# Dense logits of one layer section in a single visit, four places for row maxima, lambda's sums ahead of them

## The chip, the cores and the metric

The kernel runs on one core of one Trainium2 chip. The metric is the device time of one execution in microseconds (us). Three runs of the kernel before gave 357.63, 357.84 and 358.26 us; their median is 357.84. TensorE (PE) multiplies matrices and transposes, VectorE (DVE) and ScalarE (ACT) do the elementwise work, GpSimd (POOL) does the rotations, some square roots and small loads, and SyncE (SP) issues the loads of the weights.

## The reference

The program computes two layers (`DEPTH = 2`) of a streaming encoder on 256 tokens of width 1024. Each layer normalises its input, sends it through one input projection, mixes tokens in two groups of heads, gates, projects back, normalises and adds; then a per-layer embedding is gated and added. The group that matters here is the dense one, group B, differential attention with 4 heads and 2 maps for each head:

```python
logits = jnp.einsum('bqhcd,bshcd->bchqs', qb, k).astype(jnp.float32) * (HEAD_DIM ** -0.5)
logits = jnp.where(allowed, logits, NEG_INF)
probs = jax.nn.softmax(logits, axis=-1)
attn = (probs[:, 0] - lam * probs[:, 1]).astype(v.dtype)
...
lam = (jnp.exp(jnp.sum(lambda_q1[i] * lambda_k1[i])) - jnp.exp(jnp.sum(lambda_q2[i] * lambda_k2[i])) + lam_init)
```

Allowed keys are those of the query's chunk of 64 tokens and of the chunks before it. Group A is sparse: an indexer scores the keys, the best 64 are kept (top-k), and a softmax runs over them. The outputs are float32.

## The kernel before

**Tiling.** The 256 tokens are two row blocks of 128 (b = 0 and 1). Weights come in pieces of two 128-row slices by 512 columns, 512 KB each, called units. Every unit is split into a rounded part `w_hi` (copied by ACT) and its remainder `w_lo` (subtracted by DVE), and each product is three matmuls: hi times hi, lo times hi, hi times lo (lines 1249 to 1251). A unit and a row block make one piece ("mm") of six matmuls on PE. There are five landing places `raw` for units and ten places for the split ones; SP issues the load of a unit once `lo_done` says that the unit five before it has been split.

**Order.** `all_steps` writes one list of steps for both layers, and every engine walks the same list and takes its own share of each step, strictly in that order. Between the pieces of the projections KB, VB, QA, KA, VA, GB and GA the other steps are placed by the table `PLACE`: step kind to number of the piece behind which it stands (0 is the first piece of KB). Steps with the same number are ordered by `rank`. `HIGH` and `LOW` hold the ACT copy and the DVE remainder of each unit and are placed by `LEAD`, `PACE` and corrections in `CAST_AT`.

**The steps around the change**, for the dense group:
- `("T", "KB", b)`: four PE transposes of the keys into bank `tr`; ACT copies `k_hi`, DVE subtracts `k_lo` and so signals `tr_out`.
- `("S", n)`: logits of tasks 2n and 2n+1. S0 is row block 0 (four maps of 128 keys in each task), S1 and S2 are row block 1 (two maps of 256 keys in each). PE writes them with matmuls that contract over 64 rows (line 1182); DVE then adds the mask and takes the negated row maximum of each map (line 1000) into `neg_max`, which has two places of four columns.
- `("E", n)`: ACT takes the exponentials with that maximum as bias (line 746) and sums the rows.
- `("R", i)`: DVE turns the sums into factors and subtracts lambda times the second map from the first (lines 1010 to 1024), which signals `mix_done`.
- `("PT", n)`: PE transposes the mixed probabilities into `tr` (line 1398), ACT copies them to `pT`. `("PV", m)`: PE multiplies them with the values into `pv` (line 1415).
- `("lam",)`: DVE waits on `small_in`, which counts five small loads of POOL (four lambda vectors, line 519, and `g_sub`, line 520), multiplies and sums (lines 826 and 827), scales `g_sub` (828) and, when ACT has taken the exponentials of the sums (line 807), makes `neg_lam` (830).

In layer 0 POOL issues those five loads behind the rotation of the first key block, and behind them the loads of `p_raw`, `g_ple` and `g_norm`; in layer 1 they are issued a layer's half ahead. Each engine executes its instructions in order: whatever stands behind a waiting instruction on its engine waits too.

Of the kernel before, what the change touches and what calls it, by code (L numbers as in the profile page):

```python
# [21 lines left out]
DEPTH, SEQ, D_MODEL, D_PLE = 2, 256, 1024, 256  # L22
P = 128
# [35 lines left out]
for _i, _u in enumerate(UNITS):  # L59
# [8 lines left out]
START = 10  # L68
HOLD = 2
LEAD, PACE = 8, 1.75  # L70
CAST_AT = {39: 38, 41: 43, 43: 44}
WARM = 5
UE = KU * N


PLACE = dict(
    lam=15,
    QB=[5, 3],
    KB=[9, 12],
    QA=[25, 29],  # L80
    KA=[32, 37],
    S=[12, 15, 18, 38, 38, 44],
    E=[13, 16, 24, 38, 40, 45],
    R=[16, 16, 19, 19, 24, 24, 44, 44, 45, 45, 48, 48],
    PT=[19, 23, 26, 42, 43, 45, 46, 50, 51],
    PV=[20, 25, 28, 52, 52, 52],
    glu=46,
    hv=[21, 27],
    hn=[23, 29],
    topk=[[0, 0, 2, 6, 6, 7, 10, 11], [12, 24, 24, 25, 26, 26, 27, 31]],  # L90
    y=[51, 52, 53])

S_WITH = {1: [2], 3: [4, 5]}


def layer_steps(L):
# [27 lines left out]
    t8 = lambda src, b: [("t8", src, b, 0), ("t8", src, b, 1)]  # L124
# [23 lines left out]
        mms("QB", one(1), {2: [("TI", 1)], 3: [("D",)]})  # L148

    mid = [[] for _ in range(7 * len(both))]  # L150
    placed = [(PLACE["lam"], ("lam",)), (PLACE["glu"], ("glu", 0))]
    for kind in ("S", "E", "R", "PT", "PV"):
        placed += [(i, (kind, n)) for n, i in enumerate(PLACE[kind])]
    for kind in ("hv", "hn"):
# [3 lines left out]
    for b in range(NB):  # L158
        placed += [(i, ("topk", b, r)) for r, i in enumerate(PLACE["topk"][b])]
    placed += [(PLACE["y"][0], ("t8", "y", 0, 1)), (PLACE["y"][1], ("t8", "y", 0, 0)), (PLACE["y"][2], ("ylo", 0))]  # L160
    rank = {"glu": 0, "PV": 1, "PT": 2, "T": 3, "S": 4, "E": 5, "hv": 6, "hn": 7, "R": 8, "topk": 9,
            "lam": 10, "t8": 11, "ylo": 12}
    for i, step in sorted(placed, key=lambda q: (q[0], rank[q[1][0]], q[1][1:])):
        mid[i].append(step)
    for c, chunk in enumerate(["KB", "VB", "QA", "KA", "VA", "GB"]):
# [55 lines left out]
def build(nc, x, p, pre_norm_g, w_in, w_out, post_norm_g, lambda_q1, lambda_k1, lambda_q2, lambda_k2, subln_g,  # L221
# [6 lines left out]
    with ctx:  # L228
        def sb(name, shape, dt=fp32):
            return ctx.enter_context(nc.sbuf_tensor(name, shape, dt))  # L230
# [41 lines left out]
        lam_in = sb("lam_in", [P, 4, HEAD])  # L272
# [7 lines left out]
                        for i in range(2))  # L280
        w_idx = sb("w_idx", [P, NB, IDX_HEADS])
        top8 = sb("top8", [P, 8])
        neg_max = sb("neg_max", [P, 2, 4])
        row_sum = sb("row_sum", [P, 2, NB, 8])
        row_rec = sb("row_rec", [P, 2, NB, 8])
        mix_c = sb("mix_c", [P, 4])
# [102 lines left out]
        def tr_index(L, s):  # L389

            return L * TRN + tr_steps.index(s) + 1
# [34 lines left out]

        def s_bank(i):

            if i // 2 == 4:
                return [pv, tr][i % 2]  # L430
            return proj[2 + i % 2] if i // 2 in (2, 5) else sc[i % 2]

# [175 lines left out]
        def _(act):  # L608
# [29 lines left out]
            for pos, (L, s) in enumerate(STEPS):  # L638
# [13 lines left out]
                kind = s[0]  # L652
# [88 lines left out]
                elif kind == "E":  # L741
                    for i in (2 * s[1], 2 * s[1] + 1):
                        g, b, maps, keys = s_task(i)
                        act.wait_ge(max_done, L * 12 + i + 1)
                        for j, m in enumerate(maps):
                            last = nc.scalar.activation(probs[:, i % 4, j * keys:(j + 1) * keys],  # L746
                                                        probs[:, i % 4, j * keys:(j + 1) * keys], ACT.Exp,
                                                        bias=neg_max[:, i % 2, j:j + 1], scale=-1.0,
                                                        accum_out=row_sum[:, g, b, m:m + 1])
                        last.then_inc(exp_done, 1)  # L750
                elif kind == "PT":
# [59 lines left out]
        def _(dve):  # L811
# [4 lines left out]
            def link(ins):  # L816

                chain[0] += 1
                ins.then_inc(dve_chain, 1)
                dve.wait_ge(dve_chain, chain[0])  # L820

            def lambda_of(L):

                lam_init = 0.8 - 0.6 * math.exp(-0.3 * L)
                dve.wait_ge(small_in, 16 * 5 * (L + 1))
                link(nc.vector.tensor_tensor(lam_in[:, 0:2, :], lam_in[:, 0:2, :], lam_in[:, 2:4, :], ALU.mult))
                nc.vector.tensor_reduce(lam_s[:, :], lam_in[:, 0:2, :], AX.X, ALU.add).then_inc(lam_sum, 1)
                nc.vector.tensor_scalar(g_sub[:, :], g_sub[:, :], 1.0 - lam_init, None, ALU.mult)
                dve.wait_ge(lam_exp, L + 1)
                nc.vector.tensor_scalar(neg_lam[:, :], lam_e[:, 1:2], lam_e[:, 0:1], -lam_init, ALU.subtract, ALU.add)\  # L830
                    .then_inc(lam_done, 1)
# [11 lines left out]
            for pos, (L, s) in enumerate(STEPS):  # L843
# [136 lines left out]
                elif kind == "S":  # L980
                    for i in (2 * s[1], 2 * s[1] + 1):
                        g, b, maps, keys = s_task(i)
                        dve.wait_ge(s_done, L * 12 + i + 1)
                        if L * 12 + i >= 2:
                            dve.wait_ge(exp_done, L * 12 + i - 1)
                        if i < 4:
                            dve.wait_ge(score_done, L * 2 + i // 2 + 1)
                        elif i - 4 in PT_OF_S:

                            dve.wait_ge(tr_done, tr_index(L, ("PT", PT_OF_S[i - 4])))  # L990
                        else:
                            dve.wait_ge(mix_done, L * 3 + (i - 4) // 2 + 1)
                        if g == 1:
                            dve.wait_ge(mask_done, L * 2 + b + 1)
                            mask = sel_mask[b][:, :]
                        else:
                            mask = causal[:, SEQ - keys:SEQ]

                        for j in range(len(maps)):
                            ins = nc.vector.tensor_tensor_reduce(  # L1000
                                out=probs[:, i % 4, j * keys:(j + 1) * keys], in0=s_bank(i)[:, j * keys:(j + 1) * keys],
                                in1=mask, scale=-1.0, scalar=-TAKEN, op0=ALU.add, op1=ALU.min,
                                accum_out=neg_max[:, i % 2, j:j + 1])
                        ins.then_inc(max_done, 1)
                elif kind == "R":
                    i = s[1]
# [26 lines left out]
                elif kind == "hn":  # L1033
# [8 lines left out]
                            scale_h[:, b, h:h + 1], g_sub[:, :], ALU.mult, ALU.mult)  # L1042
                    ins.then_inc(pv_out, 1)
                elif kind == "lam":
                    lambda_of(L)
                elif kind == "post0":
                    b, n = s[1:]
# [58 lines left out]
        def _(pe):  # L1106
# [31 lines left out]
            def wait_tr(L, s):  # L1138

                i = tr_index(L, s)  # L1140
                if i > 1:
                    pe.wait_ge(tr_out, i - 1)
# [26 lines left out]
            def logits(L, n, g, b, keys):  # L1169

                for j in range(N // keys):
                    for part in range(1 if b == 0 else 3):
                        for odd in range(2):
                            m = s_task(2 * n + odd)[2][j]
                            rows = slice(odd * HEAD, (odd + 1) * HEAD)
                            if b == 0:
                                q, k = qT[g][rows, m // 2, 0:P], kT[rows, m // 2, :]
                            else:
                                q = (q_lo if part == 2 else q_hi)[rows, m // 2, :]
                                k = (k_lo if part == 1 else k_hi)[rows, m // 2, :]  # L1180
                            end = part == (0 if b == 0 else 2)
                            ins = nc.tensor.matmul(s_bank(2 * n + odd)[:, j * keys:(j + 1) * keys], q, k,  # L1182
                                                   start=(part == 0), stop=end)
                            if end and j == N // keys - 1:
                                ins.then_inc(s_done, 1)
# [16 lines left out]
            for pos, (L, s) in enumerate(STEPS):  # L1202
# [147 lines left out]
                elif kind == "D":  # L1350
# [3 lines left out]
                    for b in range(NB):  # L1354
                        keys = (b + 1) * P
                        for j in range(2):
                            for odd in range(2):
# [3 lines left out]
                                                       start=True, stop=True)  # L1361
                                if j == 1:
                                    ins.then_inc(dots_done, 1)
                elif kind == "S" and s[1] not in (2, 4, 5):
                    g, b, _, keys = s_task(2 * s[1])
                    keys_from = ("KB" if g == 0 else "KA", b)
                    if b == 0:
# [2 lines left out]
                        pe.wait_ge(tr_out, tr_index(L, ("T",) + keys_from))  # L1370
                    if s[1] == 0:
                        pe.wait_ge(relu_done, L * 4 + 4)
                    elif s[1] == 1:
                        pe.wait_ge(max_done, L * 12 + 2)
                    else:
                        pe.wait_ge(max_done, L * 12 + 4)
                    logits(L, s[1], g, b, keys)
                    if s[1] == 1:
                        pe.wait_ge(z_out, L * 8 + 2)
                        logits(L, 2, g, b, keys)  # L1380
                    elif s[1] == 3:
                        pe.wait_ge(tr_out, tr_index(L, ("T", "KA", 1)))
                        pe.wait_ge(pv_out, L * 4 + 2)
                        logits(L, 4, 1, 1, SEQ)
                        pe.wait_ge(max_done, L * 12 + 6)
                        logits(L, 5, 1, 1, SEQ)
                elif kind == "PT":
                    n = s[1]
                    g, b, tiles = pt_task(n)
                    wait_tr(L, s)  # L1390
                    if g == 0:
                        pe.wait_ge(mix_done, L * 3 + n + 1)
                    else:
                        pe.wait_ge(exp_done, L * 12 + tiles[1][2] + 1)
# [59 lines left out]
```

## Time and profile before

| | |
|---|---|
| median of three runs | 357.84 us |
| profiled execution, whole time | 358.45 us |
| its span, first to last instruction | 356.7 us |
| PE busy | 348.7 us (98%) |
| DVE busy | 263.6 us (74%) |
| ACT busy | 229.0 us (64%) |
| POOL busy | 68.0 us (19%) |
| mean granted PE clock | 0.994 of full speed |

The span covers all instructions of one execution; 1.75 us of the whole time lie around it. A busy share is an average over all stages. PE's matmuls are pipelined: a row of 0.39 us can be followed by the next start 0.23 us later, so for PE the distance between starts is the measure of what a matmul costs.

### The profile page before, as it was taken

The numbers are of one execution on the slowest core, as the hardware profiler recorded it, in microseconds if no ns is written. First come the engines' busy times: TensorE is split into PE (matmuls) and PEld (weight loads), VectorE is DVE, ScalarE is ACT, GpSimd is POOL, SyncE is SP. The second block draws the span as 40 slices with busy tenths as digits, with TensorE's granted clock in tenths as the row PEclk, the third lists the DMA queues.
The fourth block names the chain that finished last, engine by engine and source line by source line (L and its number), as shares of the span: only waits on it lengthen the run. The fifth ranks groups of instructions, "written<-read, shape, count | busy, mean of one in ns | idle before, by whom it ended". The sixth has DMA issues, their size and how long they took to land.

```text
span 356.7 us, 5705 instructions
## 1 busy us (share of the span) xinstructions
PE 348.7 (98%) x1927; PEld 292.0 (82%) x1927; DVE 263.6 (74%) x562; ACT 229.0 (64%) x459; POOL 68.0 (19%) x121
## 2 busy tenths in 40 slices
PE   8999999999999999999999999999999999999992
PEld 7897888888888788888888888788888888888882
DVE  2886979988875676786797577988895658678543
ACT  4797567686577945555667564787666796365221
POOL 1066351142200000003105624004230000000000
PEclk9999999999999999999999999999999999999997
DMA  7996479862744464657575927546356336550011
GB/s 265 380 360 191 125 224 175 285 173 67 196 160 148 146 195 159 203 167 154 182 226 155 349 82 208 161 122 180 115 146 208 115 130 228 176 169 10 2 48 69
DMA packets 31820, 61.12 MB, mean 171 GB/s; under 512 B 2376, under 2 KB 4432, under 8 KB 31792
## 3 DMA queue, kind: packets, MB, share of 16 engines
q1 hardware_dynamic: 30656, 57.48, 50.3%
q0 software_dynamic: 1120, 3.28, 4.8%
q8 instruction: 16, 0.26, 0.3%
q14 instruction: 12, 0.10, 0.1%
q10 hardware_dynamic: 16, 0.00, 0.0%
HBM read 59.71 MB, written 1.05 MB: 170 GB/s over the span
## 4 chain that ended last, share of the span: by engine, by line
PE 94%; issue 2%; DMA 1%; DVE 1%; ACT 0%; POOLq 0%; DVEq 0%; POOL 0%; SPq 0%
PE proj L1249 26%; PE proj L1251 25%; PE proj L1250 25%; PE sc L1330 3%; PE tr L1398 2%; PE tr L1348 2%; PE sc L1182 2%; PE pv L1415 1%; DMA raw<-in_w_ple_proj_dram 1%; PE proj L1166 1%; PE proj L1193 1%; PE pv L1420 1%; PE proj L1182 1%; PE proj L1262 1%; PE proj L1155 1%
## 5 line engine op out<-in xcount | busy, mean ns | idle before, releaser
L1249 PE MATMUL proj<-w_hi,act_hi 128*128 128x512 f32 (+1 forms) x392 | 157.1, 401 | 0.0
L1251 PE MATMUL proj<-w_hi,act_lo 128*128 128x512 f32 (+1 forms) x392 | 152.2, 388 | 0.0
L1250 PE MATMUL proj<-w_lo,act_hi 128*128 128x512 f32 (+1 forms) x392 | 151.6, 387 | 0.0
L849 DVE TENSOR_TENSOR w_lo<-raw,w_hi 128x1024 fp32r<-128x1024 f32 (+1 forms) x102 | 121.3, 1208 | 10.5 <-ACT w_hi L610 9.9
L610 ACT ACTIVATE w_hi<-raw 128x1024 fp32r<-128x1024 f32 (+2 forms) x103 | 102.4, 1023 | 3.3 <-PE proj L1251 1.8
L1251 PEld LDWEIGHTS proj<-w_hi,act_lo 128*128 128x128 f32 x392 | 73.6, 188 | 15.5
L1249 PEld LDWEIGHTS proj<-w_hi,act_hi 128*128 128x128 f32 x392 | 73.7, 188 | 14.3 <-issue 0.7
L1250 PEld LDWEIGHTS proj<-w_lo,act_hi 128*128 128x128 f32 x392 | 73.8, 188 | 12.8
L551 POOL TENSOR_TENSOR rstd<-var,minus_half 128x1 f32<-128x1 f32 x12 | 7.6, 639 | 190.8 <-DVE var L837 161.4
L746 ACT ACTIVATE probs<-probs,neg_max 128x128 f32<-128x128 f32 (+1 forms) x64 | 28.2, 444 | 4.8 <-DVE neg_max L1000 4.8
L541 POOL TENSOR_TENSOR v_all<-work,rot_tab 128x128 f32<-128x128 f32 x16 | 10.6, 662 | 76.8 <-ACT work L610 76.6
L610 ACT ACTIVATE act_hi<-sc 128x512 fp32r<-128x512 f32 x20 | 11.4, 600 | 17.6 <-PE sc L1330 16.0
L610 ACT ACTIVATE pT<-tr 128x512 f32<-128x512 f32 (+1 forms) x16 | 9.1, 569 | 9.9 <-PE tr L1398 6.3
L929 DVE TENSOR_TENSOR act_lo<-sc,act_hi 128x512 fp32r<-128x512 f32 x16 | 10.4, 683 | 5.8 <-ACT act_hi L610 5.8
L746 ACT ACTIVATION_READ_ACCUMULATOR probs<-probs,neg_max 128x1 f32 x64 | 12.1, 188 | 0.0
L975 DVE MAX8 top<-score 128x8 f32<-128x128 f32 (+1 forms) x32 | 11.4, 358 | 0.6
L948 DVE TENSOR_TENSOR k_lo<-tr,k_hi 128x512 fp32r<-128x512 f32 x8 | 5.5, 688 | 8.5 <-ACT k_hi L610 8.5
L976 DVE MATCH_REPLACE8 score<-top,score 128x128 f32<-128x128 f32 (+1 forms) x32 | 11.0, 343 | 0.0
L1398 PEld LDWEIGHTS tr<-ident,probs 128*128 128x128 f32 x72 | 8.8, 140 | 2.6 <-ACT work L610 0.5
L1398 PE MATMUL tr<-ident,probs 128*128 128x128 f32 x72 | 10.8, 273 | 0.0
L1065 DVE TENSOR_TENSOR work<-work,emb 128x512 f32<-128x512 f32 x7 | 4.8, 686 | 7.2 <-ACT work L782 7.2
L542 POOL TENSOR_TENSOR v_all<-work,rot_tab 128x64 f32<-128x64 f32 x16 | 10.1, 632 | 0.0
(229 smaller groups left out, 450.1 us busy)
## 6 DMA issues: line engine op xcount, KB each, us to landing
raw<-in_w_in_dram SPq DMA_DIRECT2D x59, 512.0 KB, 4.1
raw<-in_w_out_dram SPq DMA_DIRECT2D x16, 512.0 KB, 3.3
raw<-in_w_ple_gate_dram SPq DMA_DIRECT2D x16, 512.0 KB, 3.8
raw<-in_w_in_dram SPq DMA_DIRECT2D x7, 324.0 KB, 5.0
raw<-in_w_ple_proj_dram SPq DMA_DIRECT2D x4, 512.0 KB, 4.1
resid<-in_x_dram SPq DMA_DIRECT2D x2, 512.0 KB, 7.1
probs<-in_w_in_dram SPq DMA_DIRECT2D x2, 512.0 KB, 9.3
g_ple<-in_ple_norm_g_dram POOLq DMA_DIRECT2D x2, 512.0 KB, 8.0
```

Of the source, the lines that this page charges most:

```text
L541: nc.gpsimd.tensor_tensor(rot_a[:, 0:heads, :], view[:, :, 0:ROT], table(cos2, slice(0, ROT)), ALU.mult)
L610: return nc.scalar.activation(dst, src, ACT.Copy, scale=scale)
L746: last = nc.scalar.activation(probs[:, i % 4, j * keys:(j + 1) * keys], probs[:, i % 4, j * keys:(j + 1) * keys], ACT.Exp, bias=neg_max[:, ...
L849: nc.vector.tensor_tensor(w_lo[:, g % SLOTS, 0:nk * cols], landing(g, nk * cols), w_hi[:, g % SLOTS, 0:nk * cols].bitcast(fp32), ALU.subtr ...
L975: link(nc.vector.max(top8[:, :], score[b][:, :]))
L976: link(nc.vector.match_replace(score[b][:, :], top8[:, :], score[b][:, :], TAKEN))
L1182: ins = nc.tensor.matmul(s_bank(2 * n + odd)[:, j * keys:(j + 1) * keys], q, k, start=(part == 0), stop=end)
L1249: nc.tensor.matmul(ps, src_hi[:, b, k0 + k, :], hi, start=(first_u and k == 0), stop=False)
L1250: nc.tensor.matmul(ps, src_hi[:, b, k0 + k, :], lo, start=False, stop=False)
L1251: last = nc.tensor.matmul(ps, src_lo[:, b, k0 + k, :], hi, start=False, stop=last_k)
L1330: last = nc.tensor.transpose(sc[i % 2][:, j * P:(j + 1) * P], tile, ident[:, :])
L1398: last = nc.tensor.transpose(tr[:, j * P:(j + 1) * P], probs[:, si % 4, col:col + P], ident[:, :])
```

## The change

- **One visit.** PE computes the logits of all three dense steps in one go: S0 moves from place 12 to 13 and issues S1 and S2 behind its own (`S_WITH = {0: [1, 2], ...}`); S1 no longer stands at 15. S1's tasks go to the banks `pv` and `tr` instead of `sc`. The first transposition of probabilities gets a further wait, for the maxima of S1 (`max_done`), since it overwrites `tr`.
- **Maxima.** `neg_max` has four places instead of two, and DVE waits for the exponential of four tasks ago instead of two.
- **DVE and ACT.** S1's maxima stand directly behind S0's, S1's exponentials (E1) at place 14 instead of 16, the first top-k round of row block 1 at 14 instead of 12.
- **Lambda.** `lambda_of` is split. `lambda_sums` (wait on `small_in`, product, sum) is the step "lam", now at place 13 with a rank ahead of S. The rest is the step "neg" at 15. ACT's exponential of the sums stays with "lam".
- **One cast.** `CAST_AT` moves the ACT copy and the DVE remainder of one unit a place later.

```diff
-CAST_AT = {39: 38, 41: 43, 43: 44}
+CAST_AT = {15: 16, 39: 38, 41: 43, 43: 44}
-    lam=15,
+    lam=13,
+    neg=15,
-    S=[12, 15, 18, 38, 38, 44],
-    E=[13, 16, 24, 38, 40, 45],
+    S=[13, 13, 18, 38, 38, 44],
+    E=[13, 14, 24, 38, 40, 45],
...
-S_WITH = {1: [2], 3: [4, 5]}
+S_WITH = {0: [1, 2], 3: [4, 5]}
...
-            if i // 2 == 4:
+            if i // 2 in (1, 4):
                 return [pv, tr][i % 2]
...
-            def lambda_of(L):
-
-                lam_init = 0.8 - 0.6 * math.exp(-0.3 * L)
+            def lambda_sums(L):
+
                 dve.wait_ge(small_in, 16 * 5 * (L + 1))
                 link(nc.vector.tensor_tensor(lam_in[:, 0:2, :], lam_in[:, 0:2, :], lam_in[:, 2:4, :], ALU.mult))
                 nc.vector.tensor_reduce(lam_s[:, :], lam_in[:, 0:2, :], AX.X, ALU.add).then_inc(lam_sum, 1)
+
+            def lambda_of(L):
+
+                lam_init = 0.8 - 0.6 * math.exp(-0.3 * L)
                 nc.vector.tensor_scalar(g_sub[:, :], g_sub[:, :], 1.0 - lam_init, None, ALU.mult)
...
-                        if L * 12 + i >= 2:
-                            dve.wait_ge(exp_done, L * 12 + i - 1)
+                        if L * 12 + i >= 4:
+                            dve.wait_ge(exp_done, L * 12 + i - 3)
...
                     logits(L, s[1], g, b, keys)
-                    if s[1] == 1:
+                    if s[1] == 0:
+                        pe.wait_ge(tr_out, tr_index(L, ("T", "KB", 1)))
+                        logits(L, 1, 0, 1, SEQ)
                         pe.wait_ge(z_out, L * 8 + 2)
-                        logits(L, 2, g, b, keys)
+                        logits(L, 2, 0, 1, SEQ)
...
+                    if n == 0:
+                        pe.wait_ge(max_done, L * 12 + 4)
```

DVE in layer 0, before, from the remainder of the second key block on (each maximum has a second row that reads its accumulator):

```order
L948 TENSOR_TENSOR k_lo<-tr,k_hi 128x4x128 [waits qk_hi_done]
L1000 ISA probs,neg_max<-sc,causal 128x128 [waits score_done,s_done]
...
L973 MEMSET score 64x64 [waits score_done]
L975 MAX top<-score 128x8 [waits dve_chain]
L976 MATCH_REPLACE score<-top,score 128x256 [waits dve_chain]
L849 TENSOR_TENSOR w_lo<-raw,w_hi 128x1024 [waits hi_done,dve_chain]
L1000 ISA probs,neg_max<-sc,causal 128x256 [waits score_done,exp_done,s_done]
...
L826 TENSOR_TENSOR lam_in<-lam_in 128x128 [waits small_in]
L827 TENSOR_REDUCE lam_s<-lam_in 128x2 [waits dve_chain]
L828 TENSOR_SCALAR g_sub<-g_sub 128x128
L830 TENSOR_SCALAR neg_lam<-lam_e 128x1 [waits lam_exp]
```

The same engine and place with the change:

```order
L952 TENSOR_TENSOR k_lo<-tr,k_hi 128x4x128 [waits qk_hi_done]
L826 TENSOR_TENSOR lam_in<-lam_in 128x128 [waits small_in]
L827 TENSOR_REDUCE lam_s<-lam_in 128x2 [waits dve_chain]
L1004 ISA probs,neg_max<-sc,causal 128x128 [waits score_done,s_done]
...
L1004 ISA probs,neg_max<-pv,causal 128x256 [waits score_done,s_done]
...
L853 TENSOR_TENSOR w_lo<-raw,w_hi 128x1024 [waits hi_done]
L977 MEMSET score 64x64 [waits score_done]
L979 MAX top<-score 128x8 [waits dve_chain]
L980 MATCH_REPLACE score<-top,score 128x256 [waits dve_chain]
L832 TENSOR_SCALAR g_sub<-g_sub 128x128 [waits dve_chain]
L834 TENSOR_SCALAR neg_lam<-lam_e 128x1 [waits lam_exp]
```

The wait on `small_in` stood behind all maxima of S0 and S1; it now stands ahead of them.

ACT in layer 0, before, from the copy of the second key block to the first copy of transposed probabilities:

```order
L610 ACTIVATE k_hi<-tr 128x4x128 [waits tr_done]
L610 ACTIVATE w_hi<-raw 128x1024 [waits unit_used,raw_in1]
L746 ACTIVATE probs,row_sum<-probs,neg_max 128x128 [waits max_done]
...
L610 ACTIVATE w_hi<-raw 128x1024 [waits unit_used,raw_in2]
L610 ACTIVATE v_all<-proj,rstd 128x512 [waits rstd_done0,unit_used]
L807 ACTIVATE lam_e<-lam_s 128x2 [waits lam_sum]
L746 ACTIVATE probs,row_sum<-probs,neg_max 128x256 [waits max_done]
...
L610 ACTIVATE w_hi<-raw 128x1024 [waits unit_used,raw_in3]
L610 ACTIVATE w_hi<-raw 128x1024 [waits unit_used,raw_in4]
L610 ACTIVATE work<-proj,rstd 128x512 [waits rstd_done0,b0_done]
L610 ACTIVATE pT<-tr 128x512 [waits tr_done]
```

With the change:

```order
L611 ACTIVATE k_hi<-tr 128x4x128 [waits tr_done]
L611 ACTIVATE w_hi<-raw 128x1024 [waits unit_used,raw_in1]
L808 ACTIVATE lam_e<-lam_s 128x2 [waits lam_sum]
L747 ACTIVATE probs,row_sum<-probs,neg_max 128x128 [waits max_done]
...
L747 ACTIVATE probs,row_sum<-probs,neg_max 128x256 [waits max_done]
...
L611 ACTIVATE v_all<-proj,rstd 128x512 [waits rstd_done0,unit_used]
L611 ACTIVATE w_hi<-raw 128x1024 [waits unit_used,raw_in2]
L611 ACTIVATE w_hi<-raw 128x1024 [waits unit_used,raw_in3]
L611 ACTIVATE w_hi<-raw 128x1024 [waits unit_used,raw_in4]
L611 ACTIVATE work<-proj,rstd 128x512 [waits rstd_done0,b0_done]
L611 ACTIVATE pT<-tr 128x512 [waits tr_done]
```

All dense exponentials now stand ahead of the value copy and of three casts, and the exponential of the lambda sums stands ahead of them all.

## Rows read from the trace of the kernel before

**Rows 1.** Section 1 of the page: busy time, share, instructions.
```profile
PE 348.7 (98%) x1927; PEld 292.0 (82%) x1927; DVE 263.6 (74%) x562; ACT 229.0 (64%) x459; POOL 68.0 (19%) x121
```

**Rows 2.** Timeline of PE, first key transposition of layer 0: start, duration, instruction.
```profile
49.69 0.39 PE L1251 MATMUL proj<-w_hi,act_lo 128*128 128x512 f32 x1
...
50.59 0.40 PE L1250 MATMUL proj<-w_lo,act_hi 128*128 128x512 f32 x1
```

**Rows 3.** Timeline of PE, last matmul before T and S0, second behind.
```profile
54.26 0.39 PE L1251 MATMUL proj<-w_hi,act_lo 128*128 128x512 f32 x1
...
56.45 0.40 PE L1250 MATMUL proj<-w_lo,act_hi 128*128 128x512 f32 x1
```

**Rows 4.** Timeline of PE, the same two around S1 and S2.
```profile
60.09 0.39 PE L1251 MATMUL proj<-w_hi,act_lo 128*128 128x512 f32 x1
...
62.37 0.40 PE L1250 MATMUL proj<-w_lo,act_hi 128*128 128x512 f32 x1
```

**Rows 5.** Timeline of PE, the same two around S3, S4, S5 in one visit.
```profile
99.25 0.40 PE L1251 MATMUL proj<-w_hi,act_lo 128*128 128x512 f32 x1
...
102.43 0.40 PE L1250 MATMUL proj<-w_lo,act_hi 128*128 128x512 f32 x1
```

**Rows 6.** Answer on the tile g_sub, both layers: issue, time to landing.
```profile
L520 POOL DMA_DIRECT2D g_sub<-in_subln_g_dram x2: 542/543/544, 53.0 to 163.1; - x2
...
DMA to landing us min/median/max: 6.2/7.0/7.8
```

**Rows 7.** Answer on line 520, window 49 to 62 us alone.
```profile
DMA to landing us min/median/max: 7.8/7.8/7.8
```

**Rows 8.** Timeline of DVE in layer 0, S0 to the mix.
```profile
56.72 0.28 DVE L1000 CUSTOM_DVE_ANT_0 probs<-sc,causal 128x128 f32<-128x128 f32 x1
...
58.44 0.11 DVE L973 MEMSET score<- 64x64 f32 x1
...
59.57 1.23 DVE L849 TENSOR_TENSOR w_lo<-raw,w_hi 128x1024 fp32r<-128x1024 f32 x1
...
61.42 0.42 DVE L1000 CUSTOM_DVE_ANT_0 probs<-sc,causal 128x256 f32<-128x256 f32 x1 [0.62 <-PE sc L1182]
...
62.80 0.28 DVE L826 TENSOR_TENSOR lam_in<-lam_in 128x128 f32<-128x128 f32 x1
...
63.33 0.22 DVE L828 TENSOR_SCALAR g_sub<-g_sub 128x128 f32<-128x128 f32 x1
...
63.81 1.22 DVE L849 TENSOR_TENSOR w_lo<-raw,w_hi 128x1024 fp32r<-128x1024 f32 x1
64.94 0.23 DVE L1010 RECIPROCAL row_rec<-row_sum 128x4 f32<-128x4 f32 x2
...
65.86 1.14 DVE L1024 SCALAR_TENSOR_TENSOR probs<-probs,mix_c 128x128 f32<-128x128 f32 x4
```

**Rows 9.** Timeline of ACT in layer 0, E0 to the copy of PT0.
```profile
57.67 0.40 ACT L746 ACTIVATE probs<-probs,neg_max 128x128 f32<-128x128 f32 x1 [1.01 <-DVE neg_max L1000]
...
60.77 1.04 ACT L610 ACTIVATE w_hi<-raw 128x1024 fp32r<-128x1024 f32 x1
...
63.55 0.49 ACT L746 ACTIVATE probs<-probs,neg_max 128x256 f32<-128x256 f32 x1
...
65.53 1.99 ACT L610 ACTIVATE w_hi<-raw 128x1024 fp32r<-128x1024 f32 x2
67.80 0.69 ACT L610 ACTIVATE work<-proj,rstd 128x512 f32<-128x512 f32 x1 [0.29 <-PE proj L1251]
68.39 0.59 ACT L610 ACTIVATE pT<-tr 128x512 f32<-128x512 f32 x1
```

**Rows 10.** Timeline of PE in layer 0, PT0 and PV0.
```profile
67.61 0.60 PE L1398 MATMUL tr<-ident,probs 128*128 128x128 f32 x4
...
69.43 1.05 PE L1415 MATMUL pv<-v_all,pT 128*128 128x128 f32 x8
```

**Rows 11.** Timeline of DVE in layer 1, first maximum of S0.
```profile
228.18 0.28 DVE L1000 CUSTOM_DVE_ANT_0 probs<-sc,causal 128x128 f32<-128x128 f32 x1
```

More of the change, by code:

```diff
@@ L89 @@
     hn=[23, 29],
-    topk=[[0, 0, 2, 6, 6, 7, 10, 11], [12, 24, 24, 25, 26, 26, 27, 31]],
+    topk=[[0, 0, 2, 6, 6, 7, 10, 11], [14, 24, 24, 25, 26, 26, 27, 31]],
     y=[51, 52, 53])
-S_WITH = {1: [2], 3: [4, 5]}
+S_WITH = {0: [1, 2], 3: [4, 5]}
 def layer_steps(L):
@@ L150, in layer_steps @@
     mid = [[] for _ in range(7 * len(both))]
-    placed = [(PLACE["lam"], ("lam",)), (PLACE["glu"], ("glu", 0))]
+    placed = [(PLACE["lam"], ("lam",)), (PLACE["neg"], ("neg",)), (PLACE["glu"], ("glu", 0))]
     for kind in ("S", "E", "R", "PT", "PV"):
@@ L160, in layer_steps @@
     placed += [(PLACE["y"][0], ("t8", "y", 0, 1)), (PLACE["y"][1], ("t8", "y", 0, 0)), (PLACE["y"][2], ("ylo", 0))]
-    rank = {"glu": 0, "PV": 1, "PT": 2, "T": 3, "S": 4, "E": 5, "hv": 6, "hn": 7, "R": 8, "topk": 9,
-            "lam": 10, "t8": 11, "ylo": 12}
+    rank = {"glu": 0, "PV": 1, "PT": 2, "T": 3, "lam": 4, "S": 5, "E": 6, "hv": 7, "hn": 8, "R": 9, "topk": 10,
+            "neg": 11, "t8": 12, "ylo": 13}
     for i, step in sorted(placed, key=lambda q: (q[0], rank[q[1][0]], q[1][1:])):
@@ L282, in build @@
         top8 = sb("top8", [P, 8])
-        neg_max = sb("neg_max", [P, 2, 4])
+        neg_max = sb("neg_max", [P, 4, 4])
         row_sum = sb("row_sum", [P, 2, NB, 8])
@@ L747, in _ @@
                                                         probs[:, i % 4, j * keys:(j + 1) * keys], ACT.Exp,
-                                                        bias=neg_max[:, i % 2, j:j + 1], scale=-1.0,
+                                                        bias=neg_max[:, i % 4, j:j + 1], scale=-1.0,
                                                         accum_out=row_sum[:, g, b, m:m + 1])
@@ L1002, in _ @@
                                 in1=mask, scale=-1.0, scalar=-TAKEN, op0=ALU.add, op1=ALU.min,
-                                accum_out=neg_max[:, i % 2, j:j + 1])
+                                accum_out=neg_max[:, i % 4, j:j + 1])
                         ins.then_inc(max_done, 1)
@@ L1044, in _ @@
                 elif kind == "lam":
+                    lambda_sums(L)
+                elif kind == "neg":
                     lambda_of(L)
@@ L1363, in _ @@
                                     ins.then_inc(dots_done, 1)
-                elif kind == "S" and s[1] not in (2, 4, 5):
+                elif kind == "S" and s[1] not in (1, 2, 4, 5):
                     g, b, _, keys = s_task(2 * s[1])
@@ L1372, in _ @@
                         pe.wait_ge(relu_done, L * 4 + 4)
-                    elif s[1] == 1:
+                    else:
                         pe.wait_ge(max_done, L * 12 + 2)
-                    else:
-                        pe.wait_ge(max_done, L * 12 + 4)
                     logits(L, s[1], g, b, keys)
-                    if s[1] == 1:
+                    if s[1] == 0:
+                        pe.wait_ge(tr_out, tr_index(L, ("T", "KB", 1)))
+                        logits(L, 1, 0, 1, SEQ)
                         pe.wait_ge(z_out, L * 8 + 2)
-                        logits(L, 2, g, b, keys)
+                        logits(L, 2, 0, 1, SEQ)
                     elif s[1] == 3:
```

## The prediction, made before the changed kernel ran

> **What bounds the kernel now.** I read the page's busy shares first. PE is busy for 348.7 of 356.7 us [rows 1], so nearly every microsecond that PE's own work shrinks or that PE waits goes straight into the time; DVE at 74% and ACT at 64% matter only where PE waits for them. So I next laid PE's timeline of layer 0 beside those of DVE and ACT around the dense logits, and looked for two things: what a visit to the logits costs PE, and how far ahead of PE the chain from the logits to the first transposed probabilities (PT0) and their product (PV0) runs. Last I asked when the small loads land on which lambda waits, since the change lets DVE wait for them earlier. Each layer passes the place once.
>
> **Part 1, one visit instead of two (PE).** The instructions of PE are the same in number; what goes are changes between matmuls over 128 rows and those over 64. I count from the start of the last projection matmul ahead to the start of the second one behind, so every switch is inside. Before: T and S0, 54.26 to 56.45, is 2.19 us [rows 3]; S1 with S2, 60.09 to 62.37, is 2.28 us [rows 4]; together 4.47 us. With the change the second key transposition stands alone between pieces, as the first one does now: 49.69 to 50.59, 0.90 us [rows 2]. And all three logit steps stand in one visit. The trace has exactly that shape already in the sparse group, with the banks sc, pv and tr, proj in the same order: 99.25 to 102.43, 3.18 us [rows 5]. Together 4.08 us. The saving is 0.39 us in a layer, 0.78 us in both. It lies on PE's path as a whole. Its bounds: nothing, if the junction costs elsewhere what it saves here, and 0.8 us.
>
> **Part 2, the moved wait (DVE, layer 0).** This is the term that decides. Lambda's product waits for five small loads. The last of them is g_sub, issued at 53.0 us [rows 6] and landed 7.8 us later [rows 7], at 60.8 us. Before, DVE reached that wait at 62.80 [rows 8], 2 us after the landing, and never felt it. Now the wait stands directly behind k_lo, and DVE comes there when S0's first maximum started before, at 56.72 [rows 8]. It then sits idle for 4.1 us, and behind it are queued all maxima of S0 and S1, for which ACT's exponentials wait, a weight remainder, the first top-k round and the mix; PE waits for the mix at PT0. Nothing ahead of 60.8 us changes in the queue of loads, since the remainders up to k_lo keep their times and SP's loads hang on them, so I keep the landing.
>
> Here a page of the Trainium skill speaks for the move. "DMA: Bandwidth & Descriptors", in the section on the anatomy of one DMA from GpSimd, gives about 2.0 us plus bytes over 436 GB/s for such a load; as an estimate from that page the 64 KB of g_sub would be there 2.2 us after issue, about 55.2 us, and DVE would not wait at all. The trace disagrees with it here: 7.8 us in layer 0, beside large loads in flight, and 6.2 us in layer 1 [rows 6]; I go by the trace.
>
> *DVE from 60.8 us on*, with pieces of its timeline [rows 8]:
> - product and sum of lambda, 62.80 to 63.33: 0.53
> - S0's eight maxima, 56.72 to 58.44: 1.72
> - S1's four maxima, 61.42 to 62.80: 1.38
> - one weight remainder, 63.81 to 64.94: 1.13
> - memset and first top-k round, 58.44 to 59.57: 1.13
> - g_sub and neg_lam: 0.48 before (63.33 to 63.81), with a wait for ACT in it that is now long over; I take 0.3
> - the mix of S0, 64.94 to 67.00 (65.86 + 1.14): 2.06
>
> The sum is 8.25 us, so the mix is done at 69.05. PE comes to PT0 at 67.61 before [rows 10], 0.39 earlier with part 1: 67.22. It waits 1.83 us there. Had the wait stood where it was, the same chain would have begun when S0's logits are there, which I put at 57.5 (54.26 plus 0.90 for T, five matmuls of 0.23, a switch of 0.33 and 0.92 for S0): 57.5 + 7.72 = 65.2, two microseconds ahead of PE.
>
> *ACT from 60.8 us on*, with pieces of its timeline [rows 9]: 0.53 for the lambda sums and 0.95 from DVE's first maximum to ACT's first exponential (56.72 to 57.67) bring it to 62.28. E0 takes 3.10 (57.67 to 60.77), E1 1.98 (63.55 to 65.53): 67.36. Before PT0's copy there now stand the value copy and the copy of QA, 0.69 each like the row at 67.80, and three casts at 1.0 each (65.53 with 1.99 for two); then the copy of PT0 itself, 0.59. That ends at 72.3; consecutive rows overlap by some 0.1 us, so I take 72.2. PE stands at PV0 1.82 us behind PT0 (67.61 to 69.43 [rows 10]), 69.05 + 1.82 = 70.87, and waits a second time, 1.3 us. PV0 starts at 72.2 instead of 69.43: layer 0 is 2.8 us later, with its saving already in. Without the wait ACT would end that copy at about 57.5 + 0.95 + 3.10 + 1.98 + 0.69 + 3.0 + 0.69 + 0.59, 68.5, and PV0 would come at 69.04: the new order of exponentials alone costs nothing, with half a microsecond to spare. After PV0 I see no third wait: S1's mix (DVE) is done near 74 and PT1 comes over 5 us behind PV0.
>
> **Part 3, layer 1.** There g_sub is issued at 163.1 [rows 6] and DVE comes to the place at 228.18 [rows 11]; the wait is no wait. The chain starts with S0's logits, as in the case without a wait above, and hides. Layer 1 gives the saving of 0.39 us alone.
>
> **Edits that cost nothing.** Four places for maxima relax a wait; four maxima directly behind eight need them, since no exponential is done by then. The further wait of PT0 for S1's maxima stands ahead of the mix on DVE, so the mix hides it. S1's wait for k_lo: k_lo ends at about 56.8, where S0's first maximum started, PE asks for it at 57.5 behind S0; cover 0.7 us, and if it went, PE would lose that difference once a layer. The moved remainder comes about 5 us later in layer 0; nine pieces of six matmuls at 0.23 us, 12 us, stand between it and that unit's first use. POOL's and SP's instructions keep their order.
>
> **Sum.** 2.8 - 0.4 = 2.4 us on the profiled execution, 358.45 to 360.85 us (span 356.7 to 359.1). The runs' median lies 0.61 us below the profiled time; on it the forecast is 360.2 us.
>
> **Rivals.**
> 1. *No wait, faster.* If the small loads land by about 57 us in ordinary runs, only part 1 is left: 357.84 - 0.78 = 357.1 us. For it speaks the page's figure above and that the profile itself could slow small loads; against it, that the trace counts all increments of that semaphore and both layers show over 6 us. The point from which it decides: the chain hides if the landing is earlier than 67.22 - 8.25 = 59.0 us for PT0, and 69.04 - 11.4 = 57.6 us for PV0.
> 2. *A shorter wait.* If g_sub landed after 6.2 us, as in layer 1 [rows 6], at 59.2, the PV0 copy would end at 70.6: 1.2 - 0.4 = 0.8 us, 358.6 us. For it: the loads in flight could be arranged otherwise; against it: nothing ahead of them changes.
> 3. *The saving is not there.* If one visit costs what two did, the waits stay and the sum is 2.4 + 0.78, 361.0 us. Against it stand the rows of the sparse visit [rows 5].
>
> **Chances.** The forecast 0.75, with its own range 359.4 to 361.2; the first rival 0.10, the second 0.08, the third 0.07. A measurement of this kernel can tell 0.2%, 0.7 us, from no change. The first rival gives -0.22%, at that border: I give 0.07 to faster and the rest of it with a part of the second to the same, 0.08; slower has 0.85. The range that holds 8 in 10 reaches down to the second rival and up past the third: 358.6 to 361.6.
>
> **What the profile after would show.** Right: DVE idle for about 4 us ahead of line 826 in layer 0 and not in layer 1; E0's first exponential at about 62.3 instead of 57.67; PT0 at about 69 and PV0 at about 72.2; in layer 1 the same stretch 0.4 us shorter; one visit of 3.2 us to the dense logits. Wrong: if line 826 in layer 0 runs at 57 us, or if PT0 follows its neighbour matmul without a gap, part 2 has failed; if the visit takes 3.6 us, part 1 has.

## The result and the profile after

The changed kernel took 361.0 us in the median of six runs (360.09 to 362.0), the kernel before 357.84; the ratio is 1.0081, with a 95% interval of 1.0056 to 1.0106. It is slower, as forecast (360.2 us, range 358.6 to 361.6). The profiled execution took 362.0 us; its span grew from 356.7 to 360.2 us.

The page's busy share of PE hardly moved; its row of the clock has an 8 in the ninth of 40 slices (72 to 81 us), where the kernel before had a 9:

```profile
PE 349.9 (97%) x1927; PEld 292.4 (81%) x1927; DVE 263.2 (73%) x562; ACT 229.1 (64%) x459; POOL 68.0 (19%) x121
...
PEclk9999999989999999999999999999999999999998
```

The timeline of DVE in layer 0 (start, duration, instruction, in brackets the idle time before it and what ended it) answers [rows 8]:

```profile
55.97 0.68 DVE L952 TENSOR_TENSOR k_lo<-tr,k_hi 128x512 fp32r<-128x512 f32 x1
61.11 0.29 DVE L826 TENSOR_TENSOR lam_in<-lam_in 128x128 f32<-128x128 f32 x1 [4.45 <-DMA g_sub<-in_subln_g_dram]
...
61.64 0.28 DVE L1004 CUSTOM_DVE_ANT_0 probs<-sc,causal 128x128 f32<-128x128 f32 x1
...
64.70 1.22 DVE L853 TENSOR_TENSOR w_lo<-raw,w_hi 128x1024 fp32r<-128x1024 f32 x1
...
68.18 1.14 DVE L1028 SCALAR_TENSOR_TENSOR probs<-probs,mix_c 128x128 f32<-128x128 f32 x4
```

DVE stands idle for 4.45 us behind k_lo, until g_sub lands; before, that wait did not exist. The answer on g_sub's line in the window from 49 to 64 us, the one of [rows 7], gives the time from issue to landing:

```profile
L521 POOL DMA_DIRECT2D g_sub<-in_subln_g_dram x1: 544/544/544, 52.9 to 52.9; - x1
...
DMA to landing us min/median/max: 8.2/8.2/8.2
```

ACT in layer 0, which answers [rows 9]; all its exponentials stand behind the landing, and the copy of PT0 behind them and three casts:

```profile
61.76 0.20 ACT L808 ACTIVATE lam_e<-lam_s 128x2 f32<-128x2 f32 x1 [5.23 <-DVE lam_s L827]
62.60 0.40 ACT L747 ACTIVATE probs<-probs,neg_max 128x128 f32<-128x128 f32 x1 [0.64 <-DVE neg_max L1004]
...
67.67 0.66 ACT L611 ACTIVATE v_all<-proj,rstd 128x512 f32<-128x512 f32 x1
68.24 2.94 ACT L611 ACTIVATE w_hi<-raw 128x1024 fp32r<-128x1024 f32 x3
71.08 0.66 ACT L611 ACTIVATE work<-proj,rstd 128x512 f32<-128x512 f32 x1
71.65 0.57 ACT L611 ACTIVATE pT<-tr 128x512 f32<-128x512 f32 x1
```

PE in layer 0, which answers [rows 10], with its two waits:

```profile
66.86 0.39 PE L1257 MATMUL proj<-w_hi,act_lo 128*128 128x512 f32 x1
69.47 0.63 PE L1406 MATMUL tr<-ident,probs 128*128 128x128 f32 x4 [2.22 <-DVE probs L1028]
...
70.62 0.54 PE L1255 MATMUL proj<-w_hi,act_hi 128*128 128x512 f32 x1
70.95 0.63 PE L1256 MATMUL proj<-w_lo,act_hi 128*128 128x512 f32 x1
71.38 0.63 PE L1257 MATMUL proj<-w_hi,act_lo 128*128 128x512 f32 x1
72.37 1.97 PE L1423 MATMUL pv<-v_all,pT 128*128 128x128 f32 x8 [0.36 <-ACT pT L611]
74.07 0.50 PE L1255 MATMUL proj<-w_hi,act_hi 128*128 128x512 f32 x1
```

The chain that ended last, from 54 to 75 us, names the same path, first by share and then in order of time; it runs from the load through DVE and ACT to PV0, and does not touch PE in between:

```profile
by line: DMA g_sub<-in_subln_g_dram 39.2%; ACT probs L747 20.9%; issue 9.8%; PE pv L1423 9.4%; ACT w_hi L611 8.7%; DVE probs L1004 3.8%; ACT work L611 3.2%; ACT v_all L611 2.7%; ACT pT L611 2.3%; DVE lam_in L826 1.4%; PE proj L1257 1.1%; PE
...
52.85 8.23 DMA g_sub<-in_subln_g_dram
...
62.60 2.47 ACT probs L747 x13
...
71.74 0.49 ACT pT L611
```

Something is in these rows that I had not forecast. From 70.95 to 71.38 the matmuls follow each other at 0.43 us instead of 0.23, and PV0 takes 1.70 us to the next start (72.37 to 74.07) instead of 0.81 before (69.43 to 70.24). The row of the kernel before behind its PV0:

```profile
70.24 0.48 PE L1249 MATMUL proj<-w_hi,act_hi 128*128 128x512 f32 x1
```

The busy times by stretch tell why (start:end, length, busy PE, PEld, DVE, ACT, POOL, then the granted clock, the DMA share and GB/s):

```profile
66.00:70.00 4.00, 1.78 (x11) 1.27 (x10) 3.84 (x16) 4.00 (x11) 0.00 (x0) 1.00 0.48 135
70.00:71.00 1.00, 1.00 (x6) 0.78 (x6) 1.00 (x2) 1.00 (x2) 0.00 (x0) 0.86 0.08 16
71.00:72.00 1.00, 1.00 (x3) 0.29 (x1) 1.00 (x4) 1.00 (x3) 0.17 (x1) 0.50 0.49 39
72.00:74.00 2.00, 1.64 (x9) 1.66 (x8) 1.93 (x13) 0.23 (x1) 1.28 (x4) 0.50 0.89 287
74.00:76.00 2.00, 2.00 (x10) 1.68 (x10) 1.70 (x4) 1.62 (x9) 0.00 (x0) 0.97 0.57 217
```

After its wait of 2.2 us PE ran for a little over a microsecond at 1.00 (2.4 GHz), then at 0.50 (1.2 GHz) for about 3.4 us (70.7 to 74.1), and then at full speed again. The kernel before had 1.00 throughout from 60 to 76 us.

**The accounts of the profiled executions.** I count from the second key transposition of each layer, since the opening of an execution can be early or late by itself (54.49 us before, 54.34 after).
- Layer 0 to PT0: 13.12 us before, 15.13 after, 2.01 longer.
- Layer 0 to PV0: 14.94 and 18.03, 3.09 longer, so 1.08 more.
- Layer 0 to the matmul behind PV0: 15.75 and 19.73, 3.98 longer; the last 0.89 come with the lower clock under PV0.
- Layer 1 to the matmul behind PV0: 15.75 (225.95 to 241.70) and 15.38 (229.84 to 245.22), 0.37 shorter.

3.98 - 0.37 - 0.15 for the opening is 3.46 us, and the span grew by 3.5.

### The profile page after: what moved, and what is told of

It reads as the page before. It is cut to its first block, busy times and chain, and to the rows that moved or that the text cites. A ratio compares the mean times of both kernels' runs of the same rounds, so it can differ in the third digit from the quotient of the medians.

```text
span 360.2 us, 5701 instructions
## 1 busy us (share of the span) xinstructions
PE 349.9 (97%) x1927; PEld 292.4 (81%) x1927; DVE 263.2 (73%) x562; ACT 229.1 (64%) x459; POOL 68.0 (19%) x121
## 4 chain that ended last, share of the span: by engine, by line
PE 85%; DMA 5%; ACT 3%; issue 3%; POOL 1%; DVE 1%; SPq 1%; POOLq 0%; DVEq 0%; ACTq 0%
PE proj L1255 23%; PE proj L1257 23%; PE proj L1256 23%; DMA raw<-in_w_in_dram 3%; PE sc L1336 3%; DMA g_sub<-in_subln_g_dram 2%; PE tr L1406 2%; PE pv L1423 2%; PE tr L1354 2%; ACT probs L747 1%; PE pv L1428 1%; PE sc L1188 1%; PE proj L1199 1%; ACT w_hi L611 1%; PE proj L1161 1%
```

## The experiments

All but the sums alone start from the changed kernel; a ratio is to the kernel before on the same chip.

**Sums behind.** Lambda's sums, with their wait, behind the maxima and exponentials of both groups:

```diff
-    lam=13,
+    lam=14,
-    ... "T": 3, "lam": 4, "S": 5, "E": 6, "hv": 7, ...
+    ... "T": 3, "S": 4, "E": 5, "lam": 6, "hv": 7, ...
```

> The changed kernel with lambda's sums (and their wait on the small loads) at place 14, behind the maxima of S0 and S1 and behind the exponentials E0 and E1, in both layers; nothing else differs. Theory W (the wait on the small loads, now ahead of all maxima, is the whole loss): DVE reaches line 826 at about 61.4 us, after the landing at 61.1, so no wait; PT0 comes at about 67.1, PV0 at about 69.0, the granted clock stays at 1.00, both layers keep the 0.39 us of the single visit: 357.84 - 0.78 = 357.1 us. Rival V (the loss is from the new order of the exponentials and the single visit, with the wait hidden behind it): the time stays at about 361 us.

Measured: 357.3 us, ratio 0.9972 (0.9956 to 0.9988). DVE comes to the product behind all the maxima and finds the load landed (issued at 52.7 us, 8.4 us to landing, so at 61.1):

```profile
61.51 0.29 DVE L826 TENSOR_TENSOR lam_in<-lam_in 128x128 f32<-128x128 f32 x1
```

PE's timeline in layer 0 has no gap:

```profile
54.18 0.60 PE L1354 MATMUL tr<-ident,work 128*128 128x128 f32 x4
56.11 1.16 PE L1188 MATMUL sc<-kT,qT_b 64*128 64x128 f32 x16
...
66.94 0.60 PE L1406 MATMUL tr<-ident,probs 128*128 128x128 f32 x4
68.77 1.05 PE L1423 MATMUL pv<-v_all,pT 128*128 128x128 f32 x8
```

12.76 us from the transposition to PT0, 0.36 less than before. The move of one step of two small instructions decides between slower and faster. A second run gave this again:

> The kernel with lambda's sums behind S0, S1, E0 and E1 once more, beside the two others of this call: 0.997 to 0.998 of the time before, 357.1 to 357.3 us.

Measured: 357.02 us, 0.9979 (0.9960 to 0.9997).

**Loads early.** The order of PE, DVE and ACT is that of the changed kernel; only the loads come earlier:

```diff
+                if kind == "D" and L == 0:
+                    load_small(0)
                 if kind == "T" and s[1:] == ("KB", 0) and L == 0:
-                    load_small(0)
```

> The changed kernel with the order of every compute engine untouched; only GpSimd issues the five small loads of layer 0 some 10 us earlier, ahead of the rotation of the first key block. Theory W: they have landed when DVE comes to line 826 at 56.6 us, so the sums run there at once, the maxima start when S0's logits are there (57.3), and the time is 357.1 us as in the run with the sums behind. Rival V: about 361 us. If it lies between, the early sums cost something by themselves.

Measured: 357.37 us, 0.9972 (0.9954 to 0.9990). g_sub is issued at 37.8 us, 15 us earlier than in the changed kernel, lands 7.0 us later, and DVE comes to the sums and through them without a wait:

```profile
54.95 0.68 DVE L953 TENSOR_TENSOR k_lo<-tr,k_hi 128x512 fp32r<-128x512 f32 x1
55.55 0.28 DVE L827 TENSOR_TENSOR lam_in<-lam_in 128x128 f32<-128x128 f32 x1
```

With the wait taken away at its source the loss is gone, though no compute instruction moved: the wait is the loss, and the early place of the sums costs nothing by itself.

**Sums alone.** The kernel before with `lam=12`, ranked ahead of S, and the rest of lambda as "neg" at 15; two visits and two places for maxima stay.

> The kernel before with one part of the change alone: lambda's sums stand directly ahead of S0's maxima (place 12), the rest of lambda stays at 15; two visits, two places for maxima. Theory W: DVE waits until 61.1, S0's maxima end at 63.3, and since S1's logits go to the banks that they read, PE waits at S1 from 60.4 to 63.4, 3.0 us; with 0.9 us for a granted clock of 0.5 behind it, if it comes, layer 0 is 3 to 4 us later and layer 1 unchanged: 361 to 362 us. Rival V: the sums by themselves cost nothing, 357.8 us.

Measured: 363.21 us, 1.0122 (1.0083 to 1.0162). DVE waits for 5.06 us, and PE at S1, which here needs the banks that S0's maxima read:

```profile
60.94 0.29 DVE L826 TENSOR_TENSOR lam_in<-lam_in 128x128 f32<-128x128 f32 x1 [5.06 <-DMA g_sub<-in_subln_g_dram]
```
```profile
63.38 0.58 PE L1188 MATMUL sc<-k_hi,q_hi 64*128 64x256 f32 x2 [3.81 <-DVE neg_max L1004]
...
63.73 0.44 PE L1188 MATMUL sc<-k_lo,q_hi 64*128 64x256 f32 x2
```

The direction and the place are as the theory had them; the time is over its range, since PE waited 3.8 us and not 3.0 (this execution reached the second key transposition 0.9 us earlier, at 53.55, with the landing at 60.9 all the same). Behind the wait these matmuls follow each other at about 0.21 us instead of 0.12: the granted clock is 1.00 until 63.0 us and 0.50 from there to 66.4, so here it fell while PE still waited.

**Small loads first.** GpSimd waits for the five small loads before it issues the three large ones:

```diff
                     load_small(0)
+                    pool.wait_ge(small_in, 16 * 5)
                     pool.wait_ge(lo_done, LENT[-1] + 1)
```

> The changed kernel, but GpSimd issues the three large loads of layer 0 (p_raw, g_ple, g_norm, 1.25 MB) only when the five small ones have landed. Theory Q (g_sub takes 8 us because it shares the queues with these large loads behind it): it lands after 4 to 5 us, at about 57.5, the waits at PT0 and PV0 are all but gone, 357.3 us. Rival R (the weight loads of SyncE, or the loads' own latency, make it slow): it lands after 7 to 8 us as before, 360 to 361 us.

Measured: 360.66 us, 1.0061 (1.0041 to 1.0080); g_sub landed 7.7 us after its issue at 53.9. Theory Q falls: without the large loads behind it g_sub still takes as long as in the kernel before (7.8). PE has the two waits here as well, but in another proportion, and the clock did not fall in this execution:

```profile
69.98 0.63 PE L1407 MATMUL tr<-ident,probs 128*128 128x128 f32 x4 [1.75 <-DVE probs L1029]
72.89 1.13 PE L1424 MATMUL pv<-v_all,pT 128*128 128x128 f32 x8 [0.89 <-ACT pT L612]
```

**Sums between.** Lambda's sums between the maxima of S0 and those of S1:

```diff
-    for i, step in sorted(placed, key=lambda q: (q[0], rank[q[1][0]], q[1][1:])):
+    for i, step in sorted(placed, key=lambda q: (q[0], 5.5 if q[1] == ("S", 1) else rank[q[1][0]], q[1][1:])):
```

> The changed kernel with lambda's sums between the maxima of S0 and those of S1, so that only S1's maxima and, on ACT, the exponentials stand behind the wait for the small loads. Theory A (PE waits for two chains that start at the landing, DVE's to PT0 and ACT's to PV0; the longer one sets the end): DVE's chain is 1.7 us shorter, PT0 comes at about 67.7 instead of 69.5; ACT's is only 0.8 us shorter, since its exponentials still begin behind the lambda sums, and PV0 comes at about 71.5; layer 0 loses 2.5 us against the run with the sums behind, 359.8 us. Rival B (DVE's chain to PT0 is the whole loss): the loss shrinks with it to 0.6 us, 357.9 us.

Measured: 362.09 us (360.49 to 363.31), 1.0118 (1.0093 to 1.0142).

```profile
61.66 0.29 DVE L826 TENSOR_TENSOR lam_in<-lam_in 128x128 f32<-128x128 f32 x1 [2.64 <-DMA g_sub<-in_subln_g_dram]
```
```profile
68.33 0.63 PE L1406 MATMUL tr<-ident,probs 128*128 128x128 f32 x4 [1.31 <-DVE probs L1028]
72.18 1.13 PE L1423 MATMUL pv<-v_all,pT 128*128 128x128 f32 x8 [1.83 <-ACT pT L611]
...
243.94 1.13 PE L1423 MATMUL pv<-v_all,pT 128*128 128x128 f32 x8 [0.41 <-ACT pT L611]
```

The first wait shrank, the second grew, and PV0 comes as late as in the changed kernel (18.06 us behind the transposition; 18.03 there). Rival B falls: ACT's chain from the landing sets the end, and DVE's shorter one only splits the wait. My figure was 2.3 us too low. The profile shows 1.5 of it. Layer 0 lost 3.5 us to PV0 against the sums behind, where I had put 2.5; the landing was 0.5 us later than I had put it (9.0 us after issue). Layer 1 lost 0.57 us that I had not expected (the last row; 15.15 us from the transposition to PV0, 14.58 with the sums behind): there ACT's exponentials begin behind the sums too, and ACT's reserve does not cover that. The remaining 0.8 us are not explained. The profiled execution shows a clock of 1.00 in this stretch, but three of the six had a mean clock of 0.992 or 0.993 and took 362.57 to 363.31 us, the other three 360.49 to 361.62.

**Two places for maxima**, with the sums behind: `neg_max` with two places, `i % 2`, and the old wait for `exp_done`.

> The kernel with the sums behind (place 14), but with two places for row maxima and the old wait for the exponential of two tasks ago. Theory: S1's last maxima wait for the second half of E0, so DVE's chain to PT0 ends 1.7 us later than with four places, 67.0 to 67.3 us against PE's arrival at 67.0: PE waits for 0 to 0.3 us in each layer, 357.3 to 357.9 us. Rival: the four places are needed for the order to pay, and the whole gain of 0.8 us goes: 358.1 us.

Measured: 358.81 us, 1.0032 (1.0020 to 1.0044). S1's maxima wait for free places twice, 0.97 and 0.77 us, and PE waits at PT0 (the rows name no releaser; each wait ends when ACT has done four more exponentials of E0):

```profile
59.95 0.42 DVE L1004 CUSTOM_DVE_ANT_0 probs<-pv,causal 128x256 f32<-128x256 f32 x1 [0.97 <-issue]
...
61.49 0.42 DVE L1004 CUSTOM_DVE_ANT_0 probs<-tr,causal 128x256 f32<-128x256 f32 x1 [0.77 <-issue]
```
```profile
67.49 0.63 PE L1406 MATMUL tr<-ident,probs 128*128 128x128 f32 x4 [0.50 <-DVE probs L1028]
```

PT0 is 0.65 us later in each layer (13.41 us from the transposition in layer 0 and 13.40 in layer 1, against 12.76 and 12.75). That is 1.3 us, more than the whole saving of the single visit: without the four places the rest of the change makes the kernel slower even with its wait cured. My theory's 0.3 us was too low, the rival nearer.

**Second group's exponentials at 16**, with the sums behind: `E=[13, 16, 24, ...]`.

> The kernel with the sums behind, but with the second group's exponentials back at place 16, behind the value copy and a cast. Theory: where nothing waits, the order of the exponentials is hidden work, ACT ends the copy of PT0 at the same time since the same instructions stand ahead of it: 357.3 us, as with E1 at 14. Rival: E1 directly behind E0 brings part of the gain, 357.7 us or more.

Measured: 357.45 us, 0.9992 (0.9982 to 1.0001). The interval overlaps that of the sums behind a little (up to 0.9988), so the time alone does not settle it. The trace shows a wait that is not there with E1 at 14:

```profile
61.54 0.29 DVE L826 TENSOR_TENSOR lam_in<-lam_in 128x128 f32<-128x128 f32 x1 [0.55 <-DMA g_sub<-in_subln_g_dram]
```
```profile
62.19 0.20 ACT L808 ACTIVATE lam_e<-lam_s 128x2 f32<-128x2 f32 x1 [1.32 <-DVE lam_s L827]
```
```profile
68.98 1.13 PE L1423 MATMUL pv<-v_all,pT 128*128 128x128 f32 x8 [0.65 <-ACT pT L611]
```

ACT comes to the exponential of the lambda sums before g_sub has landed. With E1 ahead of it that time is filled; with E1 behind, it is idle, and PV0 waits. So the rival has it in part: E1 directly behind E0 is worth something as long as the landing is late. How much is open: in this execution g_sub took 9.4 us, the longest of all the profiles, and DVE itself waited 0.55 us for it, most of PE's 0.65. With a landing at the usual time PE would have waited about 0.1 us, an estimate from these rows.

**Both cures**, early loads and sums behind:

> The changed kernel with both cures: the small loads of layer 0 are issued some 15 us earlier and lambda's sums stand at place 14. If the wait is gone with either one, both together give nothing more: 357.0 to 357.4 us, the same ratio to before as each alone (0.9972). If a rest of the landing's spread still reached PE in the run with the sums behind alone (its ACT chain has half a microsecond to spare), this one is 0.1 to 0.4 us faster than that.

Measured: 357.64 us, 0.9993 (0.9977 to 1.0009). The profile shows no wait at PT0 or PV0 (66.41 and 68.23, 12.75 and 14.57 us behind the transposition), and its span is 355.1 us against 354.9 for the sums behind on the same chip. So both cures together add nothing, as expected, but the time is 0.2 us above the expected range and not clear of the kernel before. Four of its twelve executions took 358.68 to 359.16 us, as did two of the twelve with the sums behind (358.93 and 359.14); none of them was profiled, and what lengthened them is not known.

**The changed kernel again:**

> The changed kernel once more, on the chip of the two others of this call. Theory (two waits that begin at the landing, and a granted clock of 0.5 behind them in some executions): 360 to 362 us, executions with a mean clock of 0.990 to 0.992 slower than those with 0.995 to 0.998, by about the 0.9 us that the profile showed at PV0.

Measured: 362.24 us, 1.0113 (1.0090 to 1.0136), just over the expected range. All six executions had a mean clock of 0.990 or 0.991, so they alone hold no pair to compare. With the six of the result there are twelve: eight at 0.990 or 0.991 with 361.36 to 363.23 us, four at 0.995 to 0.998 with 360.09 to 361.26. Within the result's six, where two have the low mean, these took 361.36 and 362.0 us and the other four 360.09 to 361.26: the expected direction, in few executions. The profile shows the same fall, at 71.3 us, behind a wait of 2.24 us:

```profile
70.78 0.63 PE L1406 MATMUL tr<-ident,probs 128*128 128x128 f32 x4 [2.24 <-DVE probs L1028]
73.75 1.55 PE L1423 MATMUL pv<-v_all,pT 128*128 128x128 f32 x8
75.06 0.47 PE L1255 MATMUL proj<-w_hi,act_hi 128*128 128x512 f32 x1
```

It also shows that 0.9 us is no fixed price. The clock fell 0.5 us after PE resumed, PE came late to PV0 and waited there no more, and PV0 took 1.31 us to the next start, 0.50 longer than before and not 0.89. ACT's copy of PT0 ended 17.92 us behind the transposition, as in the first profile (17.88). The path is the same in both; what the clock adds to it was 0.89 us once and 0.5 once.

## Why the prediction was right

**Part 1, the single visit: right.** In the profile after, the transposition alone costs 0.91 us (54.11 to 55.02) and the visit 3.19 (55.94 to 59.13), 4.10 in place of 4.47: 0.37 us in a layer, forecast 0.39. The shape was read from the sparse group's rows. The kernel with the sums behind delivers the forecast of the first rival, 0.2 to 0.3% less than before; with both cures the gain was not clear of zero.

**Part 2, the wait: the mechanism right, step by step.** The landing came at 61.1 us, forecast 60.8. From there DVE's chain took 8.2 us to the end of the mix (61.11 to 69.32), forecast 8.25. ACT's copy of PT0 ended at 72.22, forecast 72.2. PV0 started at 72.37, forecast 72.2. That these ends fit to 0.2 us is partly luck: the landing was 0.3 us later than put, and ACT's chain from it 0.3 shorter, as its three casts and three copies took 4.55 us (67.67 to 72.22) and not 4.84. Both waits of PE were there. The first held PT0 back by 2.37 us (forecast 1.83) and the second PV0 by 1.08 more (forecast 1.3), of which only 0.36 shows as idle time, since PE's matmuls between them were slow. The second one sets the end, which the sums between the maxima showed.

**What the sum lacked** is the clock. I took the work behind the waits at its usual pace; in the profiled execution PV0 alone was 0.89 us slower at 0.50. Without it that execution would have grown by 2.6 us, against the 2.4 forecast. The term that was mis-sized is therefore "2.8 us" for layer 0, which was 3.98 in the profile: 0.89 of the difference is the clock, and about 0.3 the landing, which came 0.43 us later behind the transposition than I had put it.

The median is another matter. The profiled execution was the longest of the six (362.0 us), and only two of the six had the low mean clock of 0.990 or 0.991; the other four have a median of 360.66 us, still 0.5 over the forecast. So of the 0.8 us between forecast and median the clock accounts for some 0.3, and the rest has no profile. That a mean of 0.990 or 0.991 marks such a fall is an inference. All profiles have a low clock behind their last matmul (0.53 from 352 to 356 us in the kernel before), which lowers the mean too; but the kernels in which PE waits here for 0.65 us or less never had a mean below 0.994. What a fall costs stays open, as with the small loads first executions at 0.991 (360.56 to 361.27 us) lie among those at 0.994 and above (360.03 to 361.7).

**Layer 1: right.** No wait of PE, 0.37 us shorter. DVE took the sums there at 232.07 us, while PE still computed S0.

**Edits held to be free.** The early sums are (loads early). The new order of exponentials costs nothing, and with the late landing it even helps, by an amount that was not settled. Of the four places I wrote that they relax a wait and that the new order needs them, and gave no price; they are a condition, worth 1.3 us against two places with the single visit. The moved remainder never showed as a wait of PE, but it had no run of its own.

**The rivals.** The first, no wait, was wrong of this kernel and right of two kernels with one edit more, at its price. The page of the Trainium skill that spoke for it, "DMA: Bandwidth & Descriptors" in its section on a DMA from GpSimd, would have had g_sub there in some 2.2 us, an estimate from its formula; g_sub issued near 53 us took 7.7 to 9.4 us in ten profiles here, so in this kernel a price for a load by itself does not tell when it lands. The second, a shorter wait, and the third, no saving, did not come.

## What to carry to other kernels

- Before moving a step earlier, read when each thing it waits for arrives, and list what stands behind it on its in-order engine. Here two instructions of 0.5 us moved ahead of a late 64 KB load cost over 3 us, and moving only them back, or issuing the load earlier, turned a loss of 0.8 to 1.1% into a gain of 0.2 to 0.3%.
- Follow each chain that starts at the wait to the engine that sets the end. There were two, and shortening the one that ends in the first visible wait gained nothing, because the other ended later.
- When several edits come together, test which of them carries the others: the single visit pays only with the four places for maxima.

## What the runs showed of the hardware

- The granted clock of PE can fall at its waits inside a kernel that is otherwise busy throughout. In three profiles it fell from 1.00 to 0.50: 1.25 us after the end of a wait of 2.22 us, 0.5 us after the end of one of 2.24, and 0.4 us before the end of one of 3.81. It stayed at 0.50 for about 3.4 us each time. It stayed at 1.00 around the waits of 1.75 and 0.89, of 1.31 and 1.83, of 0.65, and of 0.50. These are single profiled executions.
- A load of 64 KB issued by GpSimd near 53 us took 7.7 to 9.4 us to land, whether three large loads followed it in the same queue or not. Issued near 38 us it took 7.0 and 7.4, and in layer 1, between 161 and 168 us, 5.8 to 6.6. What holds it up, the weight loads in flight, the four smaller loads issued just ahead of it or something else, was not settled.
